# Taking the two token tiles apart at the stage boundaries of a four-layer kernel on one core

## The reference

```python
# layers of the first kind (l = 0, 1)
h = rms_norm(x, norm_mix_pre[l])
x = x + rms_norm(hybrid_mixer(h, ...), norm_mix_post[l])     # 4 branches, gates, w_out
h = rms_norm(x, norm_ffn_pre[l])
x = x + rms_norm(swiglu(h, w_ffn_in[l], w_ffn_out[l]), norm_ffn_post[l])
# layers of the second kind (l = 0, 1)
x = x + mixer_2(rms_norm(x, norm_mix_2[l]))                  # 4 other branches
x = x + cross_attention(rms_norm(x, norm_xattn_2[l]), rms_norm(mem, norm_mem_2[l]))
h = rms_norm(x, norm_mlp_2[l])
x = x + square(relu(h @ w_up_2[l])) @ w_down_2[l]
y = rms_norm(x, norm_final_2)

def rms_norm(x, g):
    y = x * rsqrt(mean(x * x, axis=-1) + 1e-6)
    return y * g
```

## Time and profile before

| | |
|---|---|
| median of 3 runs | 2387.88 us |
| the profiled execution | 2388.0 us |
| its span | 2386.2 us |
| TensorE matmuls | 2311.3 us, 97% |
| VectorE | 1438.1 us, 60% |
| ScalarE | 1120.1 us, 47% |
| GpSimd | 62.1 us, 3% |
| share of the chain that ended last | TensorE 95%, ScalarE 2%, VectorE 2% |
| DMA | 370 MB, 155 GB/s |
| mean granted clock of TensorE | 0.988 |

### The profile page before, as it was taken

One profiled execution on the slowest core, in us unless ns is written; L12 is line 12 of the kernel. 1 busy time (PEld: TensorE's weight loads), 2 busy tenths in 40 slices (PEclk: granted clock), 3 DMA queues, 4 the chain that ended last, 5 costly groups with the idle time before them and its releaser, 6 DMA issues.

```text
span 2386.2 us, 38133 instructions
## 1 busy us (share of the span) xinstructions
PE 2311.3 (97%) x16700; PEld 2170.3 (91%) x16700; DVE 1438.1 (60%) x1566; ACT 1120.1 (47%) x1421; POOL 62.1 (3%) x58
## 2 busy tenths in 40 slices
PE   7999999999999999999999999999999999999998
PEld 7988998998898899899889998989978999898987
DVE  7567558445756755744677757445557775744554
ACT  4644545344454455433455444443445544444343
POOL 0000000000000000000000000000000000000000
PEclk9999999999999999999999999999999999999999
DMA  7423455555543345555545334445555443444563
GB/s 234 152 94 119 143 176 176 171 192 197 148 144 104 110 155 177 171 178 193 178 144 142 124 107 159 142 159 177 193 168 157 124 137 111 157 144 159 177 203 106
DMA packets 300153, 370.06 MB, mean 155 GB/s; under 512 B 25054, under 2 KB 267476, under 8 KB 299988
## 3 DMA queue, kind: packets, MB, share of 16 engines
q1 hardware_dynamic: 299988, 367.63, 48.6%
HBM read 366.55 MB, written 1.05 MB: 154 GB/s over the span
## 4 chain that ended last, share of the span: by engine, by line
PE 95%; ACT 2%; DVE 2%; issue 0%; POOL 0%; DMA 0%; POOLq 0%; DVEq 0%; ACTq 0%
PE ps L499 27%; PE ps L1874 21%; PE ps L2393 7%; PE ps L780 5%; PE ps L1885 4%; PE ps L520 4%; PE ps L733 4%; PE ps L1951 3%; PE ps L1934 2%; PE ps L747 2%; PE ps L660 1%; PE ps L626 1%; PE ps L2160 1%; PE ps L1900 1%; PE ps L2175 1%; PE ps L532 1%
## 5 line engine op out<-in xcount | busy, mean ns | idle before, releaser
L499 PE MATMUL ps<-a_nhi,a_wlo 128*128 128x256 f32 x1792 | 516.8, 288 | 13.4 <-DVE a_nlo L1103 5.6
L499 PE MATMUL ps<-a_nlo,a_whi 128*128 128x256 f32 x1792 | 508.2, 284 | 0.0
L499 PE MATMUL ps<-a_nhi,a_whi 128*128 128x256 f32 x1792 | 508.2, 284 | 0.0
L1029 DVE TENSOR_TENSOR a_wlo<-a_ring,a_whi 128x2048 fp32r<-128x2048 f32 x174 | 395.8, 2286 | 113.8 <-ACT a_whi L796 112.8
L2691 DVE TENSOR_TENSOR b_wlo<-b_ring,b_whi 128x2048 fp32r<-128x2048 f32 (+1 forms) x168 | 379.4, 2261 | 129.0 <-ACT b_whi L2409 128.8
L796 ACT CAST a_whi<-a_ring 128x2048 fp32r<-128x2048 f32 x174 | 331.4, 1905 | 196.4 <-PE ps L499 73.2
L2409 ACT CAST b_whi<-b_ring 128x2048 fp32r<-128x2048 f32 (+1 forms) x168 | 316.5, 1884 | 161.8 <-PE ps L2393 84.8
L1874 PE MATMUL ps<-b_nhi,b_wlo 128*128 128x256 f32 x1296 | 376.7, 291 | 11.2 <-DVE b_nlo L2730 8.7
L1874 PE MATMUL ps<-b_nhi,b_whi 128*128 128x256 f32 x1296 | 368.2, 284 | 0.0
L1874 PE MATMUL ps<-b_nlo,b_whi 128*128 128x256 f32 x1296 | 368.1, 284 | 0.0
L499 PEld LDWEIGHTS ps<-a_nhi,a_wlo 128*128 128x128 f32 x1792 | 345.2, 193 | 20.1 <-issue 13.6
(11 more groups left out here) (556 smaller groups left out, 4314.5 us busy)
## 6 DMA issues: line engine op xcount, KB each, us to landing
a_ring<-in_w_in SPq DMA_DIRECT2D x50, 1024.0 KB, 5.1
b_ring<-in_w_in SPq DMA_DIRECT2D x50, 1024.0 KB, 5.8
a_ring<-in_w_ffn_in SPq DMA_DIRECT2D x44, 1024.0 KB, 5.5
a_ring<-in_w_gate SPq DMA_DIRECT2D x32, 1024.0 KB, 5.4
b_ring<-in_w_up SPq DMA_DIRECT2D x32, 1024.0 KB, 5.5
b_ring<-in_w_down SPq DMA_DIRECT2D x32, 1024.0 KB, 4.9
a_ring<-in_w_ffn_out SPq DMA_DIRECT2D x22, 1024.0 KB, 4.9
a_ring<-in_w_branch SPq DMA_DIRECT2D x16, 1024.0 KB, 5.1
```

The costliest lines, as they stand in the source:

```text
L499: mm = T.matmul(out, w[:, k, c:c + P], x_[:, k, :], start=k == 0 and n == 0, stop=k == KD - 1 and n == 2)
L1029: nc.vector.tensor_tensor(part(wlo, h), part(ring, h), part(whi, h).bitcast(F32), ALU.subtract).then_inc(lo_ok, 1)
```

## The change

It has four pieces, which stand at all seven boundaries in one form or another.

1. **The last two row parts by tile.** Where the order was part 2 (tiles 0, 1), part 3 (tiles 0, 1), it is now parts 2 and 3 for tile 0 and then parts 2 and 3 for tile 1. Inside the last block of tile 1 TensorE turns tile 0.
2. **The chain by tile.** Each engine finishes tile 0 (output norm, statistic, scaling, hi copy, lo rest) before tile 1. The splits of the next parts (`hi(...)`, `lo(...)`) stand between its steps. Three copies of 8x128x256 become two of 128x512 for each tile.
3. **The next stage's first parts token-first.** The first parts of the next stage run for tile 0 and then for tile 1, and tile 1 is turned in between. A layer of the first kind now begins with `z` and `fv` as four parts of 4x512 (24 matmuls of 512 columns each); its other input parts keep their form, in another order, and the work at fixed part numbers moves with them, most of it by one, the convolution from parts 1 to 4 to parts 6 to 9. The first four parts of the ffn and the first two of the mlp compute tokens on the partitions, and their result is turned afterwards (`hidden_turn`, `up_turn`: four blocks of 128x128 each, 32 in all in the program).
4. **The norm's weight in the scaled copy.** The weight is broadcast to 128 partitions by DMA (`gpre1`, `gpre2`, `gpre`, 512 KB on the SBUF side), and VectorE's scaling takes it as a third operand. The mlp and the cross-attention norms keep theirs.

The core of the diff:

```diff
-        for i in range(4):
+        def out_rows(i, t):
...
+            for kk in range(2):
+                if i == 3 and t == 1 and kk == 1:
+                    turn_tile(pe.engine, l, 1, 0)
...
+        for i in range(2):
+            for t in range(NT):
+                out_rows(i, t)
+        for t in range(NT):
+            for i in range(2, 4):
+                out_rows(i, t)
...
+    def scaled(e, t, gain):
+        for c in (slice(0, D // 2), slice(D // 2, D)):
+            nc.vector.scalar_tensor_tensor(xm[:, t, c], x[:, t, c], rstd[:, e, t:t + 1], gain[:, c], ALU.mult, ALU.mult
+                                           ).then_inc(xn_ok, 1)
+    def hi_tile(act, l, e, t):
+        for j in range(2):
+            act.wait_ge(tr_ps, 4 * e + 2 * t + j + 1)
+            nc.scalar.copy(*tile_of(nhi, e, t, j)).then_inc(nhi_ok, 1)
...
+        def lead_rows(i, t):
+            for kk in range(4):
+                if i == 2 and t == 0 and kk == 2:
+                    turn_in(pe.engine, l, 1)
+                k = 4 * (i % 2) + kk
+                for j, (x_, w) in enumerate(((nlo, hi), (nhi, lo), (nhi, hi))):
+                    mm = T.matmul(ps[:, i // 2 * 2 + t, :], x_[:, k, t * P:(t + 1) * P], w[:, kk, :],
...
+        mix_squares(0)
+        hi(H_FIN)
+        x_squares(0)
+        hi(H_FIN + 1)
+        hi_tile(act.engine, l, 1, 0)
+        mix_squares(1)
         hi(H_FIN + 2)
+        x_squares(1)
+        hi_tile(act.engine, l, 1, 1)
...
-        norm_out(4, 7, 8, 6, gpost2)
+        for t in range(NT):
+            norm_out(4, t, 5 + t, 6 + t, 6, gpost2)
+            lo(H_END + 2 * t)
+            following.scale_in(dve.engine, following.layer, t)
+            following.lo_in(dve.engine, following.layer, t)
+            if t == 0:
+                lo(H_END + 1)
...
-        turned(0, 4)
-        cq_fill(CQA)
-        cq_fill(CQB)
+        for t in range(NT):
+            for h in (CQA, CQB):
+                cq_rows(h, t)
+            if t == 0:
+                turn_in(pe.engine, l, 1)
...
+        for t in range(NT):
+            for i in (2, 3):
+                residual_rows(H_WO + i, i, t)
+                if t == 1 and i == 2:
+                    mlp_turn(0)
...
+        for t in range(NT):
+            pe.wait_ge(nlo_ok, 12 + 2 * t + 2)
+            for i in range(2):
+                up_rows(i, t)
+                if t == 0 and i == 0:
+                    mlp_turn(1)
...
-            if 1 <= i <= 4:
-                convolve(2 * i - 2)
-                convolve(2 * i - 1)
+            if 6 <= i <= 9:
+                convolve(2 * i - 12)
+                convolve(2 * i - 11)
```

More of the change, by code:

```diff
@@ L754, in tensor @@
-        turned(1)
-        for h in range(H_FIN, H_DN):
+            for kk in range(2):
+                if i == 3 and t == 1 and kk == 1:
+                    turn_tile(pe.engine, l, 1, 0)
+                k = 2 * i + kk
+                for half in range(2):
+                    for j, (x_, w) in enumerate(((nlo, hi), (nhi, lo), (nhi, hi))):
+                        mm = T.matmul(ps[:, 2 * t + half, :], x_[:, k, t * P:(t + 1) * P],
+                                      w[:, kk, half * 512:(half + 1) * 512],
+                                      start=k == 0 and j == 0, stop=k == KD - 1 and j == 2)
@@ L816, in scalar, with evict_lead @@
         n_ssq = [0]
-        def turned(e, gain):
-            for k in range(KD):
-                if k % 2 == 0:
-                    act.wait_ge(tr_ps, 4 * e + k // 2 + 1)
-                S.activation(nhi[:, k, :], ps[:, 4 * e + k // 2, (k % 2) * SEQ:(k % 2 + 1) * SEQ], ACT.Copy,
-                             scale=parT[:, gain + k:gain + k + 1]).then_inc(nhi_ok, 1)
+        def evict_lead(n):
+            act.wait_ge(full, n + 1)
+            S.copy((z, fv)[n // 2][:, n % 2, :], ps[:, n, :]).then_inc(free_a, 1)
         def evict(i):
@@ new lines, in hi_in, with lo_in @@
+    def hi_in(act, l, t):
+        act = Counting(act, earlier(DEPTH, l))
+        for j in range(2):
+            act.wait_ge(tr_ps, 2 * t + j + 1)
+            nc.scalar.copy(*halves_in(nhi, t, j)).then_inc(nhi_ok, 1)
+    def lo_in(dve, l, t):
+        dve = Counting(dve, earlier(DEPTH, l))
+        for j in range(2):
+            dve.wait_ge(nhi_ok, 2 * t + j + 1)
+            out, turned = halves_in(nlo, t, j)
+            nc.vector.tensor_tensor(out, turned, nhi[:, 4 * j:4 * j + 4, t * P:(t + 1) * P].bitcast(F32), ALU.subtract
+                                    ).then_inc(nlo_ok, 1)
@@ L2650, in scalar @@
         hi(H_WK + 2)
[L2651 removed]
+        for i in range(H_WK + 1, H_UP - 2):
             if i == H_WK + 2:
@@ L3271, in gpsimd @@
                                     ).then_inc(rstd_ok, 1)
+        if following is not None:
+            for t in range(NT):
+                following.root_in(pool.engine, following.layer, t)
         if following is None:
```

884 lines of the change are left out of this document (556 added, 328 removed).

## The result

The changed kernel takes 2373.04 us (median of 4 runs, 2370.72 to 2373.99) where the kernel before takes 2388.65 (median of 4): a ratio of 0.9933, 95% interval 0.9918 to 0.9948. That is a gain of 15.6 us, inside the range on record and 6.7 us short of its forecast of 2366.3. The profiled execution is one of 2373.01 us with a span of 2371.2, so the two profiled spans differ by 15.0.

A forecast was written before the change was run, and what follows sets the result against it. TensorE, busy for 97% of the span, was taken to bound the kernel. Gains of 27.7 us less 6 for the clock gave 21.7, so 2366.3 from 2388.0; eight of ten between 2354 and 2377.

The forecast's parts named there:

- Cross-attention to mlp, 5.8 x 2: Boundary from cross-attention to mlp, in two layers: the turn takes `x` itself without a stall; 3.0 us for 8.8.
- mlp to the next layer, 3.3: Boundary at the mlp's end: no output norm, stalls 0.8, 1.7 and 0.9; with turns 5.3 us for 8.6.
- ffn entries, 2.0 each; ffn end, 4.3: Mixer to ffn, twice: 7.5 us for 9.5, stalls 3.0 and 1.5; ffn to the first kind: 6.9 for 11.2.
- ffn to the second kind, 1.7: Boundary from ffn to the second kind's layer: stalls 3.3, 3.7 and 0.8, with turns 9.7 us for 11.4.
- The clock, 6 us: TensorE's clock after five stalls of 3 us or more: three falls at 2.0 us each, taken off the gain.
- the rival in which the clock falls at every stall: Clock falls at all five long stalls, 2.0 us each plus 0.4 each for slower turning: 2372 us; chance 0.18.
- The rival without falls: No fall of the clock, as TensorE is interrupted for only 3 us: gain 27.7, 2360.3 us; chance 0.2.
- `z` and `fv`, 1.1 each: Projection in each first-kind layer: 96 matmuls of 512 columns replace 192 of 256, 21.9 us for 23.0.
- The mixer of the first kind, 0: Reordered mixer put at nothing, as VectorE runs a part ahead of TensorE; bounds -2 to +4 us.
- The start, +0.5: Program start: first weight part still lands at 9.8, first matmul near 14.6; gain 0.5 us, bounds -2 and +2.
- The slower rival's mechanism: First kind's parts 6 to 9: convolution beside the softplus lags on VectorE, 14 us lost per layer, 2394; chance 0.06.
- the late weights: Token-first parts hold their weights until tile 1 used them: 1.5 us missed at six boundaries, 2375 us; chance 0.08.

The follow-up runs named there:

- experiment 5: Changed kernel with the first weight part's split ahead of tile 0's chain at both ffn entries and both ffn ends: 2371.33 us, ratio to before 0.9927.
- experiment 2: Changed kernel with matmuls whose result is never read in TensorE's long waits at ffn entries, ffn ends and second kind's layer 0: 2370.29 us, ratio to before 0.9925.
- experiment 8: Changed kernel with layer 0's broadcast norm weight asked for behind the first weight part: one profile, first real matmul at 15.13 us; no run time given.
- experiment 6: Changed kernel with the third weight part's split moved behind tile 1's rests, only at the entry of the second kind: 2373.63 us, ratio to before 0.9936.
- experiment 3: The changed kernel run once more without an edit, for a second profile: 2372.68 us.
- experiment 4: Changed kernel with VectorE normalizing `y` ahead of the rope on `mk`, not behind it: 2371.27 us, ratio to before 0.9927.
- experiments 9: Changed kernel with the broadcast weight asked for behind the first weight part and 52 extra turns on TensorE at the start: 2372.3 us.
- experiment 10: Changed kernel with late weight and start turns, `y` ahead of the rope, earlier first split and matmuls in long waits together: 2364.08 us, ratio to before 0.9895.

## Why the prediction was right, and where its terms were not

**Cross-attention to mlp, 5.8 x 2.** Right in mechanism and nearly in size: 11.4 by taking it out, 10.7 against the kernel before, for 11.6. The step on which it rested, that the turn needs no norm and finds TensorE still busy, is in the trace with a wait of 0.23 (0.2 forecast).

**mlp to the next layer, 3.3.** 2.9 measured. The waits are 1.08, 1.04 and 0.96, for a forecast of 0.8, 1.7 and 0.9: 3.1 for 3.4 in sum, though the second was put too high by 0.7. Where the rest of the difference lies was not taken apart.

**ffn entries, 2.0 each; ffn end, 4.3.** The first wait is 3.17 for 3.0 and 3.2, the third block's 1.12 and 1.41 for 1.5 and 1.6. The entries gave 1.7 and 1.2. The ffn end is in one stretch with a mixer: 3.6 there, less the 1.1 of `z` and `fv`, and with the mixer's own 1.7 (below) given back, is 4.2. Right. The held power is there too, but it is worth 0.35 to 0.47 (experiment 5) and not the 0.55 that the prediction's 6.4 for 5.85 meant.

**ffn to the second kind, 1.7.** Wrong by its sign: 1.7 us slower. The waits were right (3.50, 3.38 and 0.96 for 3.3, 3.7 and 0.8). The step that failed is that of the clock: three falls were shared out over all boundaries, and two of the four came here, each behind a wait. With TensorE kept busy this stretch is 2.28 shorter (experiment 2), which makes it 0.6 better than before, so 1.1 us of the forecast are still missing. About half of that is in the waits: the 3.38 was shortened by the slow turn and matmuls ahead of it. In the profile of experiment 8 the clock stayed up until the second wait was over:

```profile
1201.92 1.09 PE L2071 MATMUL ps<-con,b_xm 128*128 128x128 f32 x8 [3.83 <-DVE b_xm L2064]
```

There the three waits are 3.49, 3.83 and 0.97, 8.3 for a forecast of 7.8. The other half was not taken apart. The reason that the prediction gave for the second wait, VectorE's split between new `x` and scaling, was wrong (experiment 6), though its length was right.

**The clock, 6 us.** Three falls were taken and four came in this profile, three to five in the others (experiment 3), so the number was about right; the price was too high: 3.0 us in all and not 2.0 each (experiment 2). It was taken from holes where nothing else was late. Here VectorE was late anyway, so most of a fall is time that would have been waited. The time measured lies near the rival in which the clock falls at every stall (2372), but by its mechanism, 2.0 for each fall and 0.4 for its turn, four falls would cost 9.6. The rival without falls (2360.3) had their number wrong.

**`z` and `fv`, 1.1 each.** Right: 0.227 a matmul.

**The mixer of the first kind, 0.** This is the term that cost most, and it is within its bounds (-2 to +4). In layer 0, from the end of `z` and `fv` to the output projection, the changed kernel takes 384.96 - 41.91 = 343.0. Before, with `z` and `fv` at 23.0 and the slow stretch of the start at 1.7 taken off, it was 365.8 - 24.7 = 341.1. Of the 1.9 lost, 1.2 is the wait for `y` that experiment 4 took away, and 0.2 the rest of TensorE's waits (6.1 with it, before 4.7); some 0.5 was not traced. The prediction looked for a lag of the convolution and found none; it did not look at what the reordering put ahead of `y`. In layer 1 the same count gives 973.20 - 630.42 = 342.8 for 366.1 - 25.0 = 341.1 (975.23 - 609.15, less 23.0 and the slow 2.0), 1.7 lost, so 3.6 in both.

**The start, +0.5.** It was -1.4 to the first matmul in this profile, the slow stretch behind it ran 4.0 us for 3.4, and the turn of tile 1 (0.8) now lies among the matmuls, where before it was done ahead of the first: -2.5 together, where the bound was -2. What failed is the step that left the first part's landing at 9.8: with the weight asked for ahead of it the part is cast at 12.25 here, at 10.8 at best, and at 9.1 to 9.7 with the weight behind it (experiments 8 to 10). How much of the -2.5 is chance is open.

So the forecast of 27.7 before the clock was too high by 3.0 for the start, 3.6 for the mixers and 3.1 over the boundaries, and the 6 for the clock by 3.0: 27.7 less 9.7 less 3.0 is 15.0. The reserve for the clock, twice as large as it had to be, made good 3.0 of the 9.7; to that extent the total is nearer than its terms, and that is luck. The slower rival's mechanism, a late convolution, and the late weights left no trace: no wait for either is among the longer ones of TensorE.

## What to carry to other kernels

When a stall is shortened, price the clock's fall behind it only where the engine would otherwise have worked: if the next operand is late anyway, a slow TensorE costs almost nothing, and lifting the clock gains almost nothing. Of a reordered list of instructions, read off for each wait of the bounding engine what now stands ahead of its releaser; 1.2 us twice came from one instruction behind a rope. And a boundary is won by what the next stage needs from the last: where it needs only `x`, taking the tiles apart removed the whole hole, where it needs two norms in a row it left half.

## What the runs showed of the hardware

- After an idle time of 3.17 us the clock fell in some executions and not in others of the same instructions (first ffn entry: a fall in the first profile, none in that of experiment 3), and stayed at 1.2 GHz for 3.4 us or for 6.8. With 13 matmuls of 512 columns in that time (experiment 2), or 11 in a shorter one (experiment 10), the granted clock was 1.00 there.
- Turns alone bring it up: after 52 turns and 8 of `x` the first matmuls started 0.23 us apart (experiments 9 and 10), where they start 0.43 apart without them.
- The record of the clock is not complete: in the changed kernel it reads 1.00 from 17 to 21 us, while matmuls of 512 columns start 0.43 apart, nearly twice the 0.227 of full speed.
- A GpSimd power of one column takes 0.55 us, and 0.90 to 1.03 when a VectorE split of 2048 columns runs beside it; it then ends 0.4 behind the split.
- One 4 KB row read for all 128 partitions, 512 KB, landed 6.4 to 8.0 us after it was asked for (seven profiles), as many bytes from 128 rows 5.8 us (one profile). With the broadcast asked for ahead of it the first weight part was cast at 10.8 to 12.3 us, with it asked for behind, at 9.1 to 9.7 (three profiles).
